# A two-block language-model kernel on one core: the retention's output gate by seven half products, its input mixtures and steps in another order

## What is computed

```python
def hybrid_layer(x, positions, norm_mix, w_in, conv_w, w_conv_out, ret_norm, w_ret_out, w_o, norm_mlp, w_up, w_down):
    h = rmsnorm(x, norm_mix)
    cb, cc, cu, q, k, v, g, ga, gb = jnp.split(h @ w_in, split_points, axis=-1)
    y_conv = short_conv_mixer(cb, cc, cu, conv_w, w_conv_out)      # (cb * conv3(cc * cu)) @ w_conv_out
    y_ret = retention_mixer(q, k, v, g, positions, ret_norm, w_ret_out)
    merged = jax.nn.sigmoid(ga) * y_conv + jax.nn.sigmoid(gb) * y_ret
    x = x + merged @ w_o
    h2 = rmsnorm(x, norm_mlp)
    return x + jnp.square(jax.nn.relu(h2 @ w_up)) @ w_down
```

## Time and profile before

| | |
|---|---|
| time, median of 3 runs | 2098.79 us (2098.56 to 2098.98) |
| span of the profiled execution, first to last instruction | 2097.1 us |
| what lies around that span, against the median | 1.7 us |
| PE busy | 2074.6 us, 99% of the span |
| DVE busy | 1564.8 us, 75% |
| ACT busy | 1067.8 us, 51% |
| granted TensorE clock, mean | 0.997 of full |

### The profile page before, as it was taken

One profiled execution on the slowest core, in us unless ns is written; L12 is line 12 of the kernel. 1 busy time (PEld: TensorE's weight loads), 2 busy tenths in 40 slices (PEclk: granted clock), 3 DMA queues, 4 the chain that ended last, 5 costly groups with the idle time before them and its releaser, 6 DMA issues.

```text
span 2097.1 us, 30779 instructions
## 1 busy us (share of the span) xinstructions
PE 2074.6 (99%) x12382; PEld 1869.8 (89%) x12382; DVE 1564.8 (75%) x2113; ACT 1067.8 (51%) x1522; POOL 27.3 (1%) x36
## 2 busy tenths in 40 slices
PE   9999999999999999999999999999999999999998
PEld 8888878878888899988999998888899988999997
DVE  8787785768656778866878887756778866868884
ACT  5776474646434445524555654434445534555653
POOL 0000000000000000000000000000000000000000
PEclk9999999999999999999999999999999999999999
DMA  5332222212322234432434353322234432344352
GB/s 186 111 101 100 91 81 71 91 66 84 107 85 87 81 111 136 146 111 91 121 107 118 118 162 105 107 91 81 91 101 141 145 107 91 121 115 118 114 175 83
DMA packets 63870, 227.96 MB, mean 109 GB/s; under 512 B 7216, under 2 KB 7600, under 8 KB 63600
## 3 DMA queue, kind: packets, MB, share of 16 engines
q1 hardware_dynamic: 59040, 208.83, 29.8%
q0 software_dynamic: 4544, 17.04, 4.7%
q10 hardware_dynamic: 144, 0.12, 0.0%
HBM read 223.86 MB, written 2.10 MB: 108 GB/s over the span
## 4 chain that ended last, share of the span: by engine, by line
PE 83%; DVE 3%; ACT 1%; issue 1%; DVEq 0%; ACTq 0%
PE bank L846 15%; PE bank L848 15%; PE bank L847 15%; PE bank L891 9%; PE bank L895 9%; PE bank L893 9%; PE bank L841 2%; PE bank L842 2%; PE bank L843 2%; PE bank L1100 1%; PE bank L1092 1%; ACT arena L1676 0%; PE bank L1169 0%; PE bank L1170 0%; PE bank L1168 0%
## 5 line engine op out<-in xcount | busy, mean ns | idle before, releaser
L1894 DVE TENSOR_TENSOR w_lo<-w_raw,w_hi 128x1024 fp32r<-128x1024 f32 x477 | 572.3, 1216 | 370.9 <-ACT w_hi L1271 368.9
L1271 ACT ACTIVATE w_hi<-w_raw 128x1024 fp32r<-128x1024 f32 x477 | 490.9, 1047 | 513.8 <-PE bank L848 333.1
L846 PE MATMUL bank<-h_both,w_hi 128*128 128x512 f32 x956 | 365.2, 382 | 2.0 <-DVE arena L1940 1.1
L847 PE MATMUL bank<-h_both,w_hi 128*128 128x512 f32 x956 | 362.3, 379 | 0.0
L848 PE MATMUL bank<-h_both,w_lo 128*128 128x512 f32 x956 | 362.3, 379 | 0.0
L846 PE MATMUL bank<-y_hi,w_hi 128*128 128x512 f32 x920 | 351.1, 382 | 5.4 <-DVE y_lo L1945 3.4
L848 PE MATMUL bank<-y_hi,w_lo 128*128 128x512 f32 x920 | 349.4, 380 | 0.0
L847 PE MATMUL bank<-y_lo,w_hi 128*128 128x512 f32 x920 | 349.2, 380 | 0.0
L846 PEld LDWEIGHTS bank<-h_both,w_hi 128*128 128x128 f32 x956 | 180.7, 189 | 30.1 <-issue 3.5
L847 PEld LDWEIGHTS bank<-h_both,w_hi 128*128 128x128 f32 x956 | 180.7, 189 | 25.9 <-issue 1.0
L848 PEld LDWEIGHTS bank<-h_both,w_lo 128*128 128x128 f32 x956 | 180.7, 189 | 25.6
(11 more groups left out here) (340 smaller groups left out, 3624.9 us busy)
## 6 DMA issues: line engine op xcount, KB each, us to landing
w_raw<-in_stream SPq DMA_DIRECT2D x389, 512.0 KB, 3.6
w_raw<-in_stream POOLq DMA_DIRECT2D x30, 512.0 KB, 5.4
x<-in_x_t SPq DMA_DIRECT2D x8, 256.0 KB, 6.7
out_t<-x SPq DMA_DIRECT2D x8, 256.0 KB, 2.1
arena<-in_consts POOLq DMA_DIRECT2D x1, 1024.0 KB, 5.2
w_raw<-in_stream SPq DMA_DIRECT2D x2, 256.0 KB, 4.3
arena<-in_positions POOLq DMA_DIRECT2D x1, 256.0 KB, 6.0
vec_t<-in_vecs ACTq DMA_DIRECT2D x1, 112.5 KB, 3.2
```

What stands on the lines that cost most here:

```text
L846: pe.matmul(out, w_hi[:, slot, w], streamed(a_h), start=first, stop=False)
L847: pe.matmul(out, w_hi[:, slot, w], streamed(a_l), start=False, stop=False)
L1271: A.activation(w_hi[:, slot, w], w_raw[:, chunks.raw_slot[raw], w], ACT.Copy).then_inc(hi_ready, 1)
L1894: V.tensor_tensor(w_lo[:, slot, w], src[:, w], w_hi[:, slot, w].bitcast(F32), ALU.subtract).then_inc(lo_ready, 1)
```

## The change

The gate `gb` becomes a `seven_products` step for both halves. For this the mixtures are needed in the retention already, and the `mix` step is cut into three: `sums_01` (the sums 0 and 1, with their high and low parts), `sums_23` (the sums alone) and `parts_23` (their parts). They stood before ret_proj0, with the parts 2 and 3 in `cc`. The steps of the retention are reordered, the half-1 buffers of v, g and the gated output are doubled, and the splitting of the gated output gets a step of its own, `r_split`. The last chunk of v1 is multiplied bank by bank. The scores wait bank by bank. In ret_proj0 the two rescale matmuls go from the last chunk to the second, and DVE multiplies x before it reads ret_proj's banks, not after. Cut to its core:

```diff
-    "ret_turn": SPLIT,
+    "ret_turn": {},
+    "r_split": SPLIT,
...
+REST_MIX = {"sums_01": {"act_out": DT // 2, "sums": 8, "mixes": 2, "vec": 2}, "sums_23": {"sums": 8}, "parts_23": {"mixes": 2}}
...
-        return [s("enter"), Bind("half", 0, [s("qk", 4, 1, True), v, *scores, g_, *outs]),
-                Bind("half", 1, [v]), Bind("half", 0, [turn]), Bind("half", 1, [s("qk", 4, 1), g_, *scores]),
-                Bind("half", 0, [gb]), Bind("half", 1, [*outs, gb, turn]),
-                Bind("half", 0, [s("mix", rest=True), s("ret_proj", 4, 1, led=True, **args)]), Bind("half", 1, [s("ret_proj", 4, 1)])]
+        return [s("enter"), half(0, s("qk", 4, 1, True), s("v", 4, 1, to="ret"), *scores()),
+                half(1, s("qk", 4, 1)), half(0, out()), mix("sums_01"), half(0, s("g", 4, 1, led=True), turn()),
+                half(1, *scores()), mix("sums_23"), half(1, s("v", 4, 1, to="ret", led=True, by_bank=True), out()),
+                mix("parts_23"), half(0, s("r_split")), half(1, s("g", 4, 1, led=True), turn()),
+                half(0, s("gb", 0, 1, seven=True)), half(1, s("r_split")), half(0, s("ret_proj", 4, 1, **args)),
+                half(1, s("gb", 0, 1, seven=True), s("ret_proj", 4, 1))]
...
-        return [Bind("half", 0, [*both(mixing=True), s("ga", 0, 1, seven=True), s("cb", 4, 1, owing=True)]),
+        return [Bind("half", 0, [*both(), s("ga", 0, 1, seven=True), s("cb", 4, 1, owing=True)]),
...
-                    if step.args.get("rescale") and c == step.chunks - 1:
+                    if step.args.get("rescale") and c == 1:
...
+            def first_bank():
+
+                if T.fixed["turn"] - 2 in sevens:
+                    return begin_turn()
+                pe.wait_ge(evacuated, T.value("turn", -7, 4))
+                return 4 * (T.fixed["turn"] % 2)
+
             def seven_products(step):
 
-                set_ = begin_turn()
+                set_ = first_bank() if step.kind == "gb" else begin_turn()
...
+                    if place == 1 and step.kind == "gb":
+                        pe.wait_ge(evacuated, T.value("turn", -4, 4))
...
             def ret_scores(step):
                 hh = step.args["hh"]
-                set_ = begin_turn()
+                set_ = 4 * (T.fixed["turn"] % 2)
...
                 for j in range(TT):
+                    bank_free(step, j)
...
             def ret_out(step):
...
                 for t in range(TT):
+                    if half == 1:
+                        pe.wait_ge(evacuated, T.value("turn", t + 1 - 4, 4))
...
+            def r_split(step):
                 half = T.var("half")
                 for n in range(4):
-                    act.wait_ge(evacuated, T.value("turn", n + 1, 4))
-                    hi(n, sg[:, n, :], half * 4 + n)
+                    A.activation(r_hi[half][:, n, :], sg[half][:, n, :], ACT.Copy).then_inc(a_hi, 1)
...
             def ret_proj(step):
                 half = T.var("half")
-                for n in range(4):
-                    banks(n)
-                    m = halves(m_t[:, half * 4 + n, :])
-                    V.tensor_tensor(m, product_bank(n), m, ALU.mult).then_inc(evacuated, 1)
                 if step.args.get("rescale"):
...
+                for n in range(4):
+                    banks(n)
+                    m = halves(m_t[:, half * 4 + n, :])
+                    V.tensor_tensor(m, product_bank(n), m, ALU.mult).then_inc(evacuated, 1)
...
             def mix(step):
 
                 split_ahead(step)
+                if step.args.get("rest") == "sums_23":
+                    sums_of(3, step)
+                    sums_of(2, step)
+                    return
+                if step.args.get("rest") == "parts_23":
+                    for n in (2, 3):
+                        mixed_low(step, n, T.value("sums"), T.value("mixes", n - 1))
+                    return
```

More of the change, by code:

```diff
@@ L814, in product @@
                         pe.wait_ge(lo_ready, T.value("chunk", c + 1))
+                    if step.args.get("by_bank") and c == step.chunks - 1:
+                        tokens_by_bank(slot, set_, [tile(k_at + KT * c + kt) for kt in range(KT)])
+                        continue
                     if step.args.get("apart") and c == step.chunks - 1:
@@ L900, in seven_products @@
                         mm.then_inc(bank_ready, 4)
[L902 to L906, removed]
             def mix(step):
-                T.mark["mix"] = T.value("mixes")
+                if step.args.get("rest") in (None, "sums_01"):
+                    T.mark["mix"] = T.value("mixes")
             def up(step):
@@ L926, in bank_by_bank, with tokens_by_bank @@
                         mm = pe.matmul(out, w_lo[:, slot, w], streamed(a_h), start=False, stop=kt == KT - 1)
+                    mm.then_inc(bank_ready, 1)
+            def tokens_by_bank(slot, set_, tiles):
+                for n in range(4):
+                    out, t = bank[set_ + n][:, :], slice(n * P, n * P + P)
+                    for kt, (a_h, a_l) in enumerate(tiles):
+                        w = slice(kt * 512, kt * 512 + 512)
+                        w_h, w_l = streamed(w_hi[:, slot, w]), streamed(w_lo[:, slot, w])
+                        pe.matmul(out, a_h[:, t], w_h, start=False, stop=False)
+                        pe.matmul(out, a_h[:, t], w_l, start=False, stop=False)
+                        mm = pe.matmul(out, a_l[:, t], w_h, start=False, stop=kt == KT - 1)
                     mm.then_inc(bank_ready, 1)
@@ L1333, in seven @@
                 products(1)
+                if step.kind == "gb":
+                    act.wait_ge(evacuated, T.value("turn", -4, 4))
                 keep(sum_, first)
@@ L1370, in seven @@
                     products(4)
-                    if not step.args.get("mixing"):
-                        first_out()
+                    first_out()
                     ahead(7)
@@ L1859, in emit @@
                     cb_step(step)
+                    return
+                if step.args.get("rest") == "parts_23":
+                    mix(step)
                     return
@@ L2612, in sums_of @@
             def sums_of(n, step):
-                after = {0: 0, 1: 4, 2: 0, 3: 8}[n]
+                after = {0: None, 1: 0, 2: None, 3: -4 if in_rest(step) else 4}[n]
                 for k in range(DT // 2):
@@ L2620, in sums_of @@
                         acted(k + 1)
-                    elif after:
-                        dve.wait_ge(summed, T.value("sums", after - 4 + k + 1))
+                    elif after is not None:
+                        dve.wait_ge(summed, T.value("sums", after + k + 1))
                     V.scalar_tensor_tensor(out=mixed_k(step, n, k), in0=x[:, far + k, t], scalar=gain_column(step, far + k),
@@ L2643, in mix @@
                     got(1)
-                for n in (0, 1, 3, 2) if in_rest(step) else (0, 1, 3):
+                for n in (0, 1) if in_rest(step) else (0, 1, 3):
                     sums_of(n, step)
```

151 lines of the change are left out of this document (87 added, 64 removed).

## The result

The changed kernel took 2104.7 us (median of 8 runs, 2103.6 to 2106.5) against 2098.9 us before on the same chip (2098.2 to 2100.5). The ratio is 1.0027, 95% interval 1.0018 to 1.0036: slower by 5.8 us. The forecast was 2102.1 us with a range of 2092 to 2107. The profiled execution is the shortest of the eight, with a span of 2101.8 us against 2097.1.

A forecast was written before the change was run, and what follows sets the result against it. PE was taken to bound the kernel, busy for 2074.6 of 2097.1 us. The terms -8.0 + 8.8 + 0.6 + 2.5 - 0.6 = +3.3 us on 2098.8 gave 2102.1 us, range 2092 to 2107.

The forecast's parts named there:

- the forecast's own bounds: Whole kernel: the terms as summed, 2099.5 to 2104.5 us; chance 0.42.
- the rival of the falling clock: Retention: PE's new waits lower the clock, three times 1.6 us, giving 2107 us; chance 0.10.
- The gain: Output gate products, two in each of two layers: seven-product steps cost 2.0 us less than plain ones, -8.0 us.
- The scores of half 1: Retention: PE waits for DVE's late read-out of g0 and for turn0; 4.4 us a layer, 8.8 in all.
- gb0: Gate product after out1: PE waits for DVE's read-out of g1's first bank, 0.3 us a layer, 0.6 in all.
- the rival in which gb starves: gb steps: DVE or ACT 1 us later, each of four steps pays about 0.7 us, giving 2105; chance 0.10.
- gb1 in the first layer: gb1's fourth chunk is split late, behind DVE's reciprocal, x tiles and ret_proj0's read-out: 2.5 us, bounds 1.5 and 3.5.
- v1 and out1: out1 directly after v1 by banks: no wait, up to 0.5 us.
- The small gain: Scores pairs: waiting bank by bank gives back 0.3 us a layer, -0.6 in all.
- DVE catches up: Scores: g0's reading starts with PE's last matmuls, costing under 1 us a layer; 2091 to 2094.5 us; chance 0.23.
- a clock of 1.00 throughout the retention: Sign expected in the profile after: the granted clock stays at 1.00 throughout the retention.
- The two rivals on the fast side: Scores of half 1: half of the 8.8 us goes, 2098, chance 0.13; or DVE catches up, chance 0.23.

The follow-up runs named there:

- experiment 3: Changed kernel with mixture sums moved behind the scores of half 1 and v1, and x rescaled in two parts: 2093.2 us, ratio 0.9972.
- experiment 5: Output gate's products plain again: on the changed kernel 2110.8 us, ratio 1.0046; on the kernel of experiment 3 2101.2 us, ratio 1.0008.
- Experiment 1: Changed kernel with mixtures 0 and 1 made behind the scores of half 1 and mixture 2's sums behind v1: 2096.6 us, ratio 0.9987.
- experiment 7: Changed kernel with the silu on g left out in both halves and layers: 2098.9 us, ratio 0.9995.
- experiment 8: Silu's table loaded early by one more ACT instruction: on the changed kernel 2101.1 us, ratio 1.0008; on the kernel of experiment 3 2090.3 us, ratio 0.9958.
- the fastest kernel: Kernel of experiment 3 with silu's table loaded early as well: 2090.3 us, ratio 0.9958.
- experiment 2: Changed kernel with half the rescaled x tiles made before ret_proj0's read-out and half before ret_proj1's: 2101.4 us, ratio 1.0010.
- experiment 6: Changed kernel with the scores waiting for the whole set of banks, not bank by bank: 2108.3 us, ratio 1.0041.
- experiment 4: Changed kernel with unused matmuls added to keep PE at work ahead of the second scores' and gb1's waits: 2102.9 us, ratio 1.0019.

## Why the prediction was right, and where it was short

The measured 2104.7 us lies in the range of 2092 to 2107, and slower was the way forecast. It lies 0.2 us outside the forecast's own bounds of 2099.5 to 2104.5, between the forecast and the rival of the falling clock (2107). A time slower by over 0.2% had been given a chance of 0.36, less than the 0.41 for one that can't be told from before.

**The gain** of 8.0 us is there: 1.9 us for each product (experiments 3 and 5), 7.5 in all. The spacing that the Trainium skill gives (TensorE: Matmul & The Clock Gate, Back-to-back issue gap), by which the half products would have lost 15 us, is not what these runs have: in the changed kernel it is 216 and 112 ns, as before.

**The scores of half 1** were forecast at 4.4 us a layer. v1 starts 37.36 us after the end of q,k; by the earlier trace rows out0, g0, turn0 and a pair of scores take 6.7 + 20.8 + 1.7 + 3.8 = 33.0, and 4.4 are left. The waits were forecast as 0.8, 2.5 and 0.4 us and were 0.7, 2.3 and 0.3 in the trace. Experiment 1 shows that the mixtures in DVE's queue cause them, experiments 7 and 8 that the second wait also needs silu and its table.

**gb0** was forecast at 0.3 us a layer and took 0.4 in the first and 0.1 in the second. That the size fits is luck, for the step failed: it had PE wait for DVE's read-out of g1's first bank. DVE had read that bank at 665.81 + 0.69 = 666.50 and PE began gb0 at 666.55, 1.76 us after turn1 began. In the fastest kernel it is 1.76 us as well, and behind other turns 1.67, so that this read cost 0.1 us at most. The gap of 0.27 us is before gb0's third place, and ACT's copy of a running sum ends just before it, at 672.13, late behind silu(g1) and its table load (in PE's and in ACT's timeline):

```profile
672.28 0.35 PE L927 MATMUL bank<-y_hi,w_hi 128*128 128x256 f32 x1
...
671.55 0.58 ACT L1364 ACTIVATE bank<-bank 128x512 f32<-128x512 f32 x1
```

With the table loaded early (experiment 8) the copy ends at 669.95, 1.0 us before PE's third place, and the gap is gone. The late copies had been named, but in the rival in which gb starves. **gb1 in the first layer** (2.5) waited 2.4, and experiment 2 shows that the eight x tiles cause it. **v1 and out1**, **the stream** and **POOL's transfers**, costed at nothing, show no wait. **The small gain** of 0.3 a layer is there: from the first matmul of the retention to that of the product behind the scores of half 0 it is 558.45 - 512.60 = 45.85 us, where the earlier trace rows had 559.19 - 513.10 = 46.09; and experiment 6 puts the waits bank by bank at 3.6 us in all, most of it at the half that was late.

**The sum.** The queue's part was +3.3; experiment 4 measures +3.9 in its windows. Of the 0.6 between them 0.5 are what the products give less; I show no cause for the rest. Two figures among the rivals were wrong and changed nothing: the sum of *DVE catches up* is 2091.8 to 2095.3 us, not 2091 to 2094.5, and its 30.7 us of DVE's work is not what the items add up to. They end at +29.1, in the trace at +29.2, while the read-out can start at +25.8 (experiment 3).

**The clock** is what was short. It was a rival with a chance of 0.10, by the argument that "no single wait reaches 3.41. It decides from a wait of about that size on." That step failed, and with it the sign "a clock of 1.00 throughout the retention". The clock fell behind waits of 2.3 and 2.4 us too, though not each time. In the profiled executions of all kernels here with such waits the clock fell behind 6 of 8 pairs of scores with a second wait of 2.3 us or more, and in gb1 behind 3 of 5 waits of 2.4. It fell behind none of the four pairs whose second wait was 0.2 or 1.2. The price of three times 1.6 us was too much in turn: with PE kept at work (experiment 4) the time is 1.8 to 2.2 us less. In the first layer gb1's fall cost 238.47 - 236.91 = 1.6 us, where PE has work without a gap behind it. The fall behind the second layer's scores cost 233.80 - 233.13 = 0.7 us, for it lay in part over waits. So the forecast's 2102.1 and the measured 2104.7 differ by the 1.8 to 2.2 us of the clock and the 0.6 of the sum, within what the runs resolve. The two rivals on the fast side had DVE early at g0's banks; it was late to 0.1 us as counted.

## What to carry over

Where the matrix engine is full, a cheaper product is worth its whole difference only if the elementwise engine's queue between two read-outs is shorter than the products it lies beside: add that queue up item by item before work is put into it (here DVE came to g0's banks 29.2 us after q,k where 25.8 was possible, and with silu's chain behind it that ate the gain). A wait of the matrix engine of some 2.3 us can cost more than itself, since the clock may fall behind it: price that with a chance, and by whether full work or another wait comes next. And look at what an engine does behind a wait although it needs no data: silu's table load of 1.28 us, moved ahead of it, gave 3.6 us in the changed kernel and 2.9 in the one of experiment 3.

## What the runs showed of the hardware

**The fall of the clock varies from one execution to the next.** The earlier trace rows show it behind the wait of 3.41 us. In the 13 profiled executions, all of kernels that are the same up to there and have that wait at about 162 us, it fell there in nine, and in three of these (experiments 1, 5 and 7) it stayed low for twice as long. The Trainium skill (TensorE: Matmul & The Clock Gate, What's actually happening) says of a kernel's start that the number of matmuls at the lower clock differs between runs of the same kernel; the traces here show the same of a fall within a kernel.

**That fall costs little where a wait follows.** In the four executions without it PE waits again 40 us later, for data that comes no sooner. PE's timeline in the fastest kernel (the last one above):

```profile
162.15 0.46 PE L877 MATMUL bank<-y_hi,w_hi 128*128 128x512 f32 x1 [3.40 <-DVE y_lo L2016]
...
202.52 0.45 PE L877 MATMUL bank<-y_hi,w_hi 128*128 128x512 f32 x1 [1.28 <-DVE y_lo L2016]
```

Of the 1.6 us lost by the clock 1.3 would have been waited for anyway. From the matmul behind the first wait to the retention's first it takes 350.6 us in these four executions, 350.7 to 350.8 in the six with a short fall, and 351.8 to 352.0 in the three with a long one. So a short slow stretch ahead of a wait is nearly free, and what is longer than the wait, or lies ahead of full work, is not.

**A table load took 1.28 us, with nothing behind it that ACT had to wait out.** The first silu begins 0.02 us after its end, and the load 0.1 us after g0's first bank was read. In experiment 8, where ACT works until 606.65, the load begins at 606.67 and the next activation at 607.97. The Trainium skill (ScalarE: Activation LUTs, What ACT_TABLE_LOAD costs) gives the same 1283 ns and a drain of some 1380 ns more; no drain shows in this trace. Before out0's root (593.07, above) stands no load, as the prediction had it: the last function with a table was a root as well.
